# Stick-breaking's cumulated sums over logarithms as one-pass fp32r matmuls of a high and a low part, the second group one tile later

## What is computed

```python
def stick_breaking_attention(q, k, v):
    ...
        valid = (kpos[None, :] < qpos[:, None]) & (kpos[None, :] >= pad)
        z = jnp.einsum('bqhd,bkhd->bhqk', q_blk, k) * scale
        log_beta = jax.nn.log_sigmoid(z)
        log_1m_beta = jnp.where(valid, jax.nn.log_sigmoid(-z), 0.0)
        log_stick = lax.cumsum(log_1m_beta, axis=3, reverse=True) - log_1m_beta
        a = jnp.where(valid, jnp.exp(log_beta + log_stick), 0.0)
        return jnp.einsum('bhqk,bkhd->bqhd', a, v)
```

## Time and profile before

| | |
|---|---|
| median of three runs | 1111.03 us (1110.56 to 1111.17) |
| the profiled execution | 1110.44 us, span 1108.5 us |
| granted TensorE clock, mean | 0.999 |
| busy PE / DVE / ACT | 1091.3 / 703.4 / 544.5 us |
| DMA | 180.02 MB, mean 162 GB/s |
| HBM read / written | 177.05 / 1.71 MB |

### The profile page before, as it was taken

The page is one execution under the profiler, slowest core; times in us unless marked ns, Lnnn a source line. Parts: engine busy times, 40 slices in busy tenths (PEclk is TensorE's granted clock), DMA queues, the critical chain, the costliest instruction groups (busy, mean ns, idle before and its releaser), DMA issues.

```text
span 1108.5 us, 19363 instructions
## 1 busy us (share of the span) xinstructions
PE 1091.3 (98%) x8597; PEld 1060.2 (96%) x8597; DVE 703.4 (63%) x770; ACT 544.5 (49%) x633; POOL 1.6 (0%) x13
## 2 busy tenths in 40 slices
PE   9999999999999999999999999999999999999998
PEld 8999999999988999999999999999999899999986
DVE  6755654588996667665547665564477867666542
ACT  5544343466545655433445534344465766544441
POOL 0000000000000000000000000000000000000000
PEclk9999999999999999999999999999999999999999
DMA  9566556857741445555453655555653244556551
GB/s 320 181 188 181 178 171 160 161 111 184 162 150 38 128 143 186 167 176 174 160 188 126 194 186 169 164 176 176 191 172 119 77 143 157 182 180 199 168 171 39
DMA packets 173072, 180.02 MB, mean 162 GB/s; under 512 B 7508, under 2 KB 165804, under 8 KB 172988
## 3 DMA queue, kind: packets, MB, share of 16 engines
q1 hardware_dynamic: 172668, 177.66, 53.3%
q10 hardware_dynamic: 320, 1.11, 0.3%
HBM read 177.05 MB, written 1.71 MB: 161 GB/s over the span
## 4 chain that ended last, share of the span: by engine, by line
PE 88%; DVE 7%; ACT 3%; issue 1%; DMA 1%; ACTq 0%; DVEq 0%
PE ps L1772 24%; PE ps L1774 23%; PE ps L1773 23%; PE ps L1877 4%; PE ps L1862 2%; PE ps L1861 2%; PE ps L1860 2%; PE ps L1995 2%; PE ps L1806 1%; PE ps L1809 1%; DVE w_lo L1153 1%; PE ps L1810 1%; PE ps L1844 1%; DVE hT L1202 1%; DVE yT L1201 1%
## 5 line engine op out<-in xcount | busy, mean ns | idle before, releaser
L1772 PE MATMUL ps<-u_hi,w_hi 128*128 128x272 f32 (+1 forms) x1656 | 479.9, 290 | 3.1 <-DVE w_lo L1153 1.2
L1774 PE MATMUL ps<-u_hi,w_lo 128*128 128x272 f32 (+1 forms) x1656 | 476.4, 288 | 0.0
L1773 PE MATMUL ps<-u_lo,w_hi 128*128 128x272 f32 (+1 forms) x1656 | 474.4, 286 | 0.0
L1153 DVE TENSOR_TENSOR w_lo<-raw,w_hi 128x2048 fp32r<-128x2048 f32 (+2 forms) x167 | 369.5, 2235 | 113.8 <-ACT w_hi L704 113.8
L704 ACT ACTIVATE w_hi<-raw 128x2048 fp32r<-128x2048 f32 (+2 forms) x167 | 310.6, 1869 | 168.2 <-PE ps L1774 143.7
L1772 PEld LDWEIGHTS ps<-u_hi,w_hi 128*128 128x128 f32 x1656 | 311.9, 188 | 5.5 <-ACT attn L967 1.2
L1773 PEld LDWEIGHTS ps<-u_lo,w_hi 128*128 128x128 f32 x1656 | 311.9, 188 | 0.3
L1774 PEld LDWEIGHTS ps<-u_hi,w_lo 128*128 128x128 f32 x1656 | 311.9, 188 | 0.0
L1772 PE MATMUL ps<-hid_hi,w_hi 128*128 128x272 f32 x528 | 152.1, 288 | 0.0
L1773 PE MATMUL ps<-hid_lo,w_hi 128*128 128x272 f32 x528 | 152.0, 288 | 0.0
L1774 PE MATMUL ps<-hid_hi,w_lo 128*128 128x272 f32 x528 | 151.5, 287 | 0.0
(11 more groups left out here) (350 smaller groups left out, 1053.0 us busy)
## 6 DMA issues: line engine op xcount, KB each, us to landing
raw<-ffn_w_up SPq DMA_DIRECT2D x44, 1024.0 KB, 5.4
raw<-ffn_w_gate SPq DMA_DIRECT2D x43, 1024.0 KB, 5.4
raw<-ffn_w_down SPq DMA_DIRECT2D x24, 896.0 KB, 4.9
raw<-ffn_w_down SPq DMA_DIRECT2D x20, 1024.0 KB, 5.2
raw<-ab_w_in SPq DMA_DIRECT2D x16, 1024.0 KB, 14.2
raw<-cd_w_in SPq DMA_DIRECT2D x9, 1024.0 KB, 5.4
raw<-ab_w_out SPq DMA_DIRECT2D x4, 1024.0 KB, 7.4
raw<-cd_w_out SPq DMA_DIRECT2D x4, 1024.0 KB, 5.1
```

What stands on the lines that cost most here:

```text
L1153: dve.tensor_tensor(dst, src, w_hi[:, n % NW, 0:rows(n) * CB].bitcast(F32), ALU.subtract)\
L1772: pe.matmul(o, wh, rhs_hi[:, kk, tok], start=first and kk == 0, stop=False)
L1773: pe.matmul(o, wh, rhs_lo[:, kk, tok], start=False, stop=False)
L1774: ins = pe.matmul(o, wl, rhs_hi[:, kk, tok], start=False, stop=last and kk == rows(n) - 1)
```

## The change

`lm` is no longer multiplied in f32. ACT copies it to `lm_hi` (fp32r, in the place of zs), DVE subtracts to `lm_lo` (fp32r, in the place of lm). The masks are copied once to fp32r (`ones_r`, `lower_r`). Each product of `stick_sums` becomes two. `log_hi` and `log_lo` are put into the queues of ACT and DVE, and on PE `stick_sums(1)` moves behind the second half of chunk 7. `stick_sums(x)` now waits for `s_lm` >= 2x + 2, that is for `log_lo(x)`.

```diff
@@ tiles @@
+        ones_r = sb("ones_r", [P], F32R)
+        lower_r = sb("lower_r", [P], F32R)
+        zs_place = place[0]
         zs = [sb("zs_0", [4, SBW]), sb("zs_1", [4, SBW])]
+        lm_hi = [at("lm_hi_0", [P, 4, SBW], F32R, zs_place), at("lm_hi_1", [P, 4, SBW], F32R, zs_place + 16 * SBW)]
         lb = [sb("lb_0", [4, SBW]), sb("lb_1", [4, SBW])]
+        lm_place = place[0]
+        lm_lo = [at("lm_lo_0", [P, 4, SBW], F32R, lm_place), at("lm_lo_1", [P, 4, SBW], F32R, yT_place)]
@@ ACT @@
+                def log_hi(x):
+                    act.wait_ge(s_lm, 2 * x + 1)
+                    act.activation(lm_hi[x][:, :, :], lm[x][:, :, :], ACT.Copy).then_inc(s_sp, 1)
+
                 for n in range(4, 8):
                     hi(b + n)
+                act.activation(ones_r[:, :], ones[:, :], ACT.Copy)
+                act.activation(lower_r[:, :], masks[:, LOWER, :], ACT.Copy)
                 stick_scores(0)
                 softplus(0)
                 hi(b + 8)
                 stick_scores(1)
                 softplus(1)
+                log_hi(0)
                 hi(b + 9)
+                log_hi(1)
                 stick_exp(0)
@@ DVE @@
+                def log_lo(x):
+
+                    dve.wait_ge(s_lm, 2 * x + 1)
+                    dve.wait_ge(s_sp, 3 + x)
+                    dve.tensor_tensor(lm_lo[x][:, :, :], lm[x][:, :, :], lm_hi[x][:, :, :].bitcast(F32), ALU.subtract)\
+                        .then_inc(s_lm, 1)
...
                 stick_log_rest(0)
                 lo(b + 8)
                 evac(6)
+                log_lo(0)
                 stick_log_beta(1)
                 stick_log_rest(1)
                 evac(7)
                 stick_exponents(0)
+                log_lo(1)
@@ PE @@
-                    pe.wait_ge(s_lm, x + 1)
+                    pe.wait_ge(s_lm, 2 * x + 2)
                     pe.wait_ge(s_aw, 1) if x else pe.wait_ge(s_zc, 2)
                     for h in range(4):
                         for j, i in ((0, 0), (0, 1), (1, 1)):
                             q0, q1 = SB_TILES[j][1], SB_TILES[i][1]
-                            mm(ps[:, 4 + h, offs[j] + q1 - q0:offs[j] + T - q0],
-                               masks[:, LOWER, :] if i == j else ones[:, :],
-                               lm[x][:, h, offs[i]:offs[i] + T - q1], i == j, i == 1)
-                    for bank, w in ((4, ones[:, :]), (5, masks[:, LOWER, :])):
-                        ins = mm(ps[:, bank, SBW:SBW + 4 * N_META], w, lm[x][:, :, offs[2]:SBW])
+                            for part in (lm_hi, lm_lo):
+                                mm(ps[:, 4 + h, offs[j] + q1 - q0:offs[j] + T - q0],
+                                   lower_r[:, :] if i == j else ones_r[:, :], part[x][:, h, offs[i]:offs[i] + T - q1],
+                                   i == j and part is lm_hi, i == 1 and part is lm_lo)
+                    for bank, w in ((4, ones_r[:, :]), (5, lower_r[:, :])):
+                        for part in (lm_hi, lm_lo):
+                            ins = mm(ps[:, bank, SBW:SBW + 4 * N_META], w, part[x][:, :, offs[2]:SBW],
+                                     part is lm_hi, part is lm_lo)
                     ins.then_inc(s_cum, 1)
@@ PE, the order @@
                 window_scores(1)
+                chunk_tile(7, 1)
                 stick_sums(1)
-                chunk_tile(7, 1)
                 pe.wait_ge(s_aw, 2)
```

More of the change, by code:

```diff
@@ L173, in build @@
         hT = sb("hT", [KD, T])
+        yT_place = place[0]
         yT = sb("yT", [KD, T])
@@ L448, in build @@
         s_zc = sem("stick_scores_copied")
-        s_sp = sem("stick_softplus_ready")
-        s_lm = sem("stick_logs_ready")
+        s_sp = sem("stick_softplus_or_hi_split")
+        s_lm = sem("stick_logs_or_lo_split")
         s_cum = sem("stick_cumulated")
```

## The result

The changed kernel takes 1115.24 us (median of six runs, 1114.28 to 1115.59), the kernel before, run beside it, 1110.97 us: 4.3 us or 0.38% slower, ratio 1.0038 with a 95% interval of 1.0028 to 1.0048. I had forecast 1113.9 with a range of 1112.7 to 1118.0. The profiled execution of the changed kernel took 1115.24 us as well, with a span of 1113.4. That is 4.9 us more than the span before; the medians differ by less, 4.3, mostly because the profiled execution before lay 0.5 us under its median.

The account below looks back on a forecast made before the run. PE, busy 98% of the span, bounds the kernel, with DVE also full in this stage. 3.1 us saved on PE against waits of 2.15, 1.2 and 2.6 gives 2.9 more: 1111.03 + 2.9 = 1113.9 us, range 1112.7 to 1118.0.

Parts of the forecast that it names:

- the three waits: PE stands before first window scores (2.15 us), second scores (1.2) and value transposes (2.6), released by DVE.
- the DVE chain: DVE in stick-breaking: low split starts 845.9, chunk 6 evacuation ends 853.8 instead of 851.3, `window_max(0)` starts 858.1.
- the first two waits: PE waits for the chunk 6 evacuation before first window scores, 2.15 us, and for `window_max(0)` before second, 1.2 us.
- The move uncovers the second exponents: Tile (7, 1) runs before the second sums, so nothing covers the exponents; PE waits 2.6 us before value transposes.
- The price of a short fp32r matmul: In PE's sums, 0.085 us per record under 256 columns, making 2.7 us per group; bounds 2.2 and 3.2.
- The rival that short fp32r matmuls are slow: PE sums: fp32r below 256 columns costs as much as f32, sums 5.5 us, 6.7 us slower, 1117.7; chance 0.3.
- the one in which each product makes two records: PE sums: masks read as f32 or two records per product, sums about 8.5 us, about 1124 us; chance 0.02.
- The clock: PE's granted clock could fall for a stretch after standing still: one or two us more, inside the range.
- My check by PE's own time: On PE, 3.1 us saved against added waits of 2.15, 1.2 and 2.6 us: 2.9 us later.
- ACT's mask copies: `ones_r` and `lower_r` ahead of `stick_scores(0)` delay ACT's logarithm chain by 0.3 us each, 0.6 in all.
- The low split: On DVE, each `log_lo` pass takes 1.9 us.
- the main case: Whole kernel at 1113.9 us, stretch 1112.8 to 1115.0, with sums between 2.2 and 3.2 us; chance 0.5.

Follow-up runs that it names:

- move without passes: Changed kernel with both low splits on DVE left out, products reading the high part twice, move kept: 1113.8 us, ratio 1.0023.
- the move alone: Kernel before, f32 sums and no split, with only the second sums put behind the second half of chunk 7: 1116.06 us, ratio 1.0050.
- The filler: Changed kernel plus nine unneeded f32 matmuls of 128 columns on PE behind the second sums: 1113.73 us.
- the kernel with the split on GpSimd: Changed kernel with the low parts made by GpSimd instead of DVE and the second sums in their old place: 1114.05 us, ratio 1.0023.
- the kernel with shortened sums: Changed kernel with 12 of the 16 144-column records per group of sums cut to 16 columns: 1119.19 us in a single execution.

## Why the prediction held, and where it was off

The direction, the three waits, their releasers and the DVE chain were right. Point by point:

- *The queue of DVE sets the first two waits.* Shown: with the passes gone (move without passes) the waits of 1.3 and 1.1 us are gone. The first was forecast as 2.15 us: the sums ended 0.45 later and the evacuation 0.2 earlier than I had put them, and the trace counts the wait from the end of the last record, not from the start that a next one could have had. The second score start was 859.30 for a forecast of 859.4.
- *The move uncovers the second exponents.* Shown twice: the move alone costs 5.3 us against the kernel before (1116.06 for an expected 1115.7), and without the move the loss of the whole change goes from 4.3 to 1.1 us. I forecast a wait of 2.6, it was 2.44.
- *The price of a short fp32r matmul* was mis-sized: 0.085 us against a measured 0.107 for the narrow records, so sums of 3.15 us and not 2.7. I took two f32 records with 64 columns as the nearest, but their weights had been loaded beside the wider records ahead of them (in the kernel before, the loads around them start 0.12 apart: 852.56, 852.68, 852.80). The records with 8 columns, all alike, gave 0.1075 and 3.2 us, my upper bound. That is also what the Trainium skill's rule on weight loads (TensorE: Matmul & The Clock Gate, LDWEIGHTS) gives, so here the Trainium skill was right and my choice against it wrong. Only the second sums lie on the path, which makes 0.4 us. Half of that was hidden by luck: the DVE chain ran 0.2 us ahead of my forecast (second scores at 859.30, less the 0.14 of the stage, for 859.4).
- *The rival that short fp32r matmuls are slow* is out: one record each, at 0.107 us and not 0.24. So is the one in which each product makes two records.
- *The clock* was the larger error, 1.64 us. I named it and left it out of the predicted time. My check by PE's own time had found a wait of 2.6 us; the step that failed is that I let PE start again at full speed behind it. The remark on the clock had no chance and no term in the sum. The filler shows the cause, the move alone that one such wait can suffice.
- *ACT's mask copies* were put at 0.3 us each; they take 0.2 (828.78, 828.98, then the scores at 829.18). *The low split* cost its 1.9.

The forecast of 2.9, with 0.4 more for the sums, 0.2 less for DVE and 1.64 for the clock, becomes 4.7; with the 0.14 of earlier stages that is the 4.9 by which the spans differ. The medians differ by 4.3, as the execution profiled before was 0.5 us low. The measured 1115.24 lies inside the range of 1112.7 to 1118.0, but in neither of the two stretches that the range was made of, 1112.8 to 1115.0 for the main case and 1116.5 to 1118.2 for slow matmuls. The prediction had said that a fall of the clock would stay inside the range, and it did; the main case had no term for it.

## What to carry to other kernels

When an edit takes time from one engine and gives work to another, read the timeline of the second one first: here 2.2 us less on PE were paid with 3.8 us more on a DVE queue that idled for 2.08 us ahead of the first exponents and 1.12 ahead of the second. A step that is moved behind other work loses that work as cover: whatever another engine computes from its result used to run beside it and now makes the first engine wait. Count that wait, and look at the granted clock behind it. And take the price of a small matmul from a run of like ones, not from the first that follows a large one.

## What the runs showed of the hardware

- One stretch of 2.44 us without a matmul was followed by 3.4 us of granted clock 0.50 (1.2 GHz) in the profiled executions of three kernels (the changed one, the move alone, the move without passes), and by none when it was filled with matmuls that nobody needed. A wait of 1.3 us and one of 1.1 us in the kernel without the move were followed by none, nor were those of 1.8 and 2.1 us in the kernel with the split on GpSimd. In the one execution of the kernel with shortened sums the clock fell behind a wait of 1.30 us and again behind one of 2.43, each time for 6.8 us; why is open.
- A matmul of 16 or 144 columns with 128 columns of new fp32r weights costs 0.11 us in a row of such.
- A GpSimd subtraction on 128 x 1728 elements takes 3.9 us. Beside it a DVE subtraction with two SBUF inputs took 5.51 us for 1.96 and a DVE copy of eight elements 2.97 for 0.17, while a DVE addition that reads PSUM took its usual 0.28.
